# Row gathers ahead of writes, a zeroing transfer, mixer activations, output tiles and weight remainders at other places in one three-layer kernel

## The reference, cut to what matters

```python
# first block
sh1, sc1, gt1, sh2, sc2, gt2 = split(silu(c) @ w_ada + b_ada, 6)
h = rms_norm(x, g_mix) * (1 + sc1) + sh1
z = h @ w_in                                       # 1024 -> conv, LRU, attention parts
u = silu(layer_norm(causal_dw_conv(cv_v * sigmoid(cv_g), 31 taps)))        # 256 wide
r = rg_lru(causal_dw_conv(lr_x, 4 taps)) * gelu(lr_y)                      # 384 wide
o = rms_norm(gla_chunked(q, k, v, log_sigmoid(g) / 16)) * silu(og)         # 4 heads of 96
x = x + gt1 * (concat(u, r, o) @ w_out)
h = rms_norm(x, g_ffn) * (1 + sc2) + sh2
x = x + gt2 * hier_moe(h)     # best of 4 groups, top 2 of its 4 experts; SwiGLU of width 512
x = rms_norm(x, g_final)
# second block, twice
x = x + 0.5 * swiglu(rms_norm(x))                  # width 2816
qa, ka, va, qs, ks, vs, zg = split(rms_norm(x) @ w_in)
o_na = neighbourhood_attention(norm(qa), norm(ka), va)      # 8 heads of 64
o_sw = sliding_window_gqa(norm(qs), norm(ks), vs, sink)     # 8 heads, 2 of keys
g = sigmoid(zg + b_gate)
x = x + (g[0] * (o_na @ w_branch_na) + g[1] * (o_sw @ w_branch_sw)) @ w_out
x = x + 0.5 * swiglu(rms_norm(x))
```

## Time and profile before

| | |
|---|---|
| three executions | 3095.05, 3088.95, 3094.0 us (median 3094.0) |
| profiled execution | 3086.77 us, its span 3085.0 us |
| mean granted TensorE clock | 0.961 |
| PE busy | 2838.5 us, 92% of the span |
| PE weight load, DVE, ACT, POOL busy | 2421.5, 1970.5, 1457.9, 136.6 us |
| chain that ended last | PE 72%, issue 9%, DVE 8%, ACT 5%, DMA 4%, POOL 2% |
| largest DMA issues | raw x220 and m_raw x192 of 512 KB, 3.3 and 6.5 us to landing |

### The profile page before, as it was taken

The page is one execution under the profiler, slowest core; times in us unless marked ns, Lnnn a source line. Parts: engine busy times, 40 slices in busy tenths (PEclk is TensorE's granted clock), DMA queues, the critical chain, the costliest instruction groups (busy, mean ns, idle before and its releaser), DMA issues.

```text
span 3085.0 us, 46431 instructions
## 1 busy us (share of the span) xinstructions
PE 2838.5 (92%) x16210; PEld 2421.5 (78%) x16210; DVE 1970.5 (64%) x2847; ACT 1457.9 (47%) x2190; POOL 136.6 (4%) x76
## 2 busy tenths in 40 slices
PE   5989869999599998999999999999998999999999
PEld 3765557777399986777889998899876777889987
DVE  7532167887589754454369975899654544479964
ACT  3251337777455433554345543655334553355532
POOL 2430200110000000000000000000000000000000
PEclk8998969999799999999999999999998999999999
DMA  7710239998222233111323223232223112323322
GB/s 288 278 41 1 96 120 339 362 355 327 100 98 99 93 102 116 41 48 48 110 89 108 98 93 116 77 108 98 88 89 116 44 38 75 103 96 110 103 82 101
DMA packets 95245, 377.60 MB, mean 122 GB/s; under 512 B 10832, under 2 KB 11104, under 8 KB 92896
## 3 DMA queue, kind: packets, MB, share of 16 engines
q1 hardware_dynamic: 89072, 348.69, 32.4%
q0 software_dynamic: 4608, 16.78, 1.4%
q10 hardware_dynamic: 1456, 10.66, 0.9%
HBM read 363.50 MB, written 16.78 MB: 123 GB/s over the span
## 4 chain that ended last, share of the span: by engine, by line
PE 72%; issue 9%; DVE 8%; ACT 5%; DMA 4%; POOL 2%; ACTq 0%; SPq 0%; DVEq 0%; POOLq 0%
PE pb L1305 11%; PE pb L1306 11%; PE pb L1307 11%; PE pb L1634 9%; PE pb L1636 9%; PE pb L1635 9%; DMA rows<-h_rows,h_idx 3%; PE pb L1830 2%; PE pb L1801 2%; PE pb L1378 1%; POOL w_lo L566 1%; PE pb L1814 1%; ACT SP L1186 1%; DMA m_raw<-in_moe_stream 1%; DVE SP L2615 1%
## 5 line engine op out<-in xcount | busy, mean ns | idle before, releaser
L1634 PE MATMUL pb<-bl,g_wh 128*128 128x256 f32 x2464 | 703.4, 285 | 30.2 <-DVE bl L2384 14.4
L1635 PE MATMUL pb<-bh,g_wl 128*128 128x256 f32 x2464 | 699.2, 284 | 0.0
L1636 PE MATMUL pb<-bh,g_wh 128*128 128x256 f32 x2464 | 699.1, 284 | 0.0
L1634 PEld LDWEIGHTS pb<-bl,g_wh 128*128 128x128 f32 x2464 | 474.9, 193 | 35.2 <-issue 24.3
L1635 PEld LDWEIGHTS pb<-bh,g_wl 128*128 128x128 f32 x2464 | 475.0, 193 | 1.8 <-issue 1.7
L1636 PEld LDWEIGHTS pb<-bh,g_wh 128*128 128x128 f32 x2464 | 474.9, 193 | 0.0
L1305 PE MATMUL pb<-hl,w_hi 128*128 128x512 f32 (+1 forms) x688 | 287.9, 419 | 49.8 <-DVE hl L1944 17.6
L624 ACT ACTIVATE w_hi<-raw 128x1024 fp32r<-128x1024 f32 x196 | 206.0, 1054 | 219.6 <-PE pb L1307 192.6
L2421 DVE TENSOR_TENSOR w_lo<-raw,w_hi 128x1024 fp32r<-128x1024 f32 x164 | 200.5, 1223 | 144.6 <-ACT w_hi L624 143.4
L1306 PE MATMUL pb<-hh,w_lo 128*128 128x512 f32 (+1 forms) x688 | 275.4, 400 | 0.0
L1307 PE MATMUL pb<-hh,w_hi 128*128 128x512 f32 (+1 forms) x688 | 275.0, 400 | 0.0
(11 more groups left out here) (420 smaller groups left out, 5445.8 us busy)
## 6 DMA issues: line engine op xcount, KB each, us to landing
raw<-in_wstream SPq DMA_DIRECT2D x220, 512.0 KB, 3.3
m_raw<-in_moe_stream SPq DMA_DIRECT2D x192, 512.0 KB, 6.5
g_own<-in_gu_stream SPq DMA_DIRECT2D x44, 768.0 KB, 4.2
raw<-in_gu_stream SPq DMA_DIRECT2D x44, 768.0 KB, 4.2
ada_ring<-in_ada SPq DMA_DIRECT2D x8, 2048.0 KB, 8.4
g_own<-in_gu_stream SPq DMA_DIRECT2D x44, 256.0 KB, 3.1
hidf<-in_gu_stream SPq DMA_DIRECT2D x44, 256.0 KB, 3.1
adaw<-in_ada SPq DMA_DIRECT2D x4, 2048.0 KB, 23.2
```

The lines of the kernel that those rows point to most:

```text
L1634: pe.matmul(o, lh, rl, start=first and k == 0, stop=False, skip_group_check=True)
L1635: pe.matmul(o, ll, rh, start=False, stop=False, skip_group_check=True)
L1636: m = pe.matmul(o, lh, rh, start=False, stop=k == 3, skip_group_check=True)
```

## The change

Six edits, none of which adds or drops a computation.

1. POOL: `put(E - 3)` stands behind `gather(E)` where `put(E - 2)` stood, so each gather is issued before the write that stood ahead of it.
2. SP: the zeroing transfer is issued after the load of chunks 22 and 23, not before that of chunk 16.
3. ACT: the z loop is written out, and sigmoid, silu and gelu stand in its iterations 6, 7 and 8.
4. DVE: `u_pad` is made ahead of the wait for the end of the projection and of the first LRU convolution.
5. PE: the `w_out` product takes its tiles in `MIX_ORDER` (LRU, linear attention, convolution), with a wait for each tile; the first tile takes bank 0 last. `w_out` is laid out to match in DRAM.
6. DVE, second block: remainders of weights stand at other places among the norms, and `scores(3)` stands ahead of a remainder.

```diff
+MIX_ORDER = (*range(NU, NMIX), *range(NU))
@@ SP
+            stream((ADA - ADA1) // ADA_EACH, C_WOUT // 2 + 1)
             sp.dma_start(y_rows[0:2 * T, :], moe_stream[...]...).then_inc(y_zero, 16)
-            stream((ADA - ADA1) // ADA_EACH, C_L // 2)
+            stream(C_WOUT // 2 + 1, C_L // 2)
@@ POOL
                 gather(E)
-                if E >= 2:
-                    put(E - 2)
-            for E in range(NE - 2, NE):
+                if E >= 3:
+                    put(E - 3)
+            for E in range(NE - 3, NE):
                 put(E)
@@ ACT
-            with act.Fori(0, NZ // 2) as j:
+            for j in range(NZ // 2):
                 for s in range(2):
...
+                if j >= 6:
+                    for s in range(2):
+                        act.wait_ge(z_evac[s], 1 + 7)
+                    at, n, function = ((Z_CG, NU, ACT.Sigmoid), (Z_OG, GH, ACT.Silu), (Z_LY, NR, ACT.Gelu_apprx_tanh))[j - 6]
+                    act.activation(z[:, at:at + n, :], z[:, at:at + n, :], function).then_inc(z_act, 1)
...
-            for s in range(2):
-                act.wait_ge(z_evac[s], 1 + 11)
-            act.activation(z[:, Z_CG:Z_CG + NU, :], z[:, Z_CG:Z_CG + NU, :], ACT.Sigmoid).then_inc(z_act, 1)
...
@@ PE
-            pe.wait_ge(mix_lo, 2 + GH)
-            for i in range(NMIX):
+            for i, tile in enumerate(MIX_ORDER):
                 s = i % 2
                 chunk(C_WOUT // 2 + i // 2, s)
-                r = slice(0, DV if i >= NU + NR else P)
-                for m in range(KD):
-                    ins = mm3(pb[m][:], w_hi[s][r, m, :], w_lo[s][r, m, :], mixh[r, i, :], mixl[r, i, :],
+                pe.wait_ge(mix_lo, 2 + GH if tile < NU else max(1, tile - NU - NR + 2))
+                r = slice(0, DV if tile >= NU + NR else P)
+                for m in (*range(1, KD), 0) if i == 0 else range(KD):
+                    if i == 0 and m == 0:
+                        pe.wait_ge(ln_act, 2)
+                    ins = mm3(pb[m][:], w_hi[s][r, m, :], w_lo[s][r, m, :], mixh[r, tile, :], mixl[r, tile, :],
@@ DVE, mixer
-            dve.wait_ge(z_evac[0], 1 + 5)
-            dve.wait_ge(z_evac[1], 1 + 5)
+            dve.memset(u_pad[:, :, 0:CONV_K - 1], 0.0).then_inc(u_ready, 1)
+            dve.wait_ge(z_act, 1)
+            dve.tensor_tensor(u_pad[...], z[:, Z_CV:Z_CV + NU, :], z[:, Z_CG:Z_CG + NU, :],
+                              ALU.mult).then_inc(u_ready, 1)
             dve.wait_ge(w_used, C_WIN + N_WIN)
-            dve.memset(u_pad[:, :, 0:CONV_K - 1], 0.0).then_inc(u_ready, 1)
             for t in range(NR):
-                if t == 1:
-                    dve.wait_ge(z_act, 1)
-                    dve.tensor_tensor(u_pad[...], z[:, Z_CV:Z_CV + NU, :], z[:, Z_CG:Z_CG + NU, :],
-                                      ALU.mult).then_inc(u_ready, 1)
@@ DVE, attention
                 low(kb + 1, 0)
+                low(kb + 1, 1)
                 qk(n0, htmp[:, 0, :], root[:], ksn[:], False).then_inc(ks_done, 1)
...
-                low(kb + 1, 1)
                 low(hb + 1, 0)
+                low(hb + 1, 1)
                 normed_q(n0 + 1)
-                low(hb + 1, 1)
+                normed_k(n0 + 1)
                 low(hb + 2, 0)
-                normed_k(n0 + 1)
...
                     normed(2)
+                    scores(3)
                     low(pr + 2, 1)
-                    scores(3)
                     normed(3)
@@ layout of w_out
-    parts = [win, wout, blocks_k(pad_to(rt, D, P))[None]]
+    parts = [win, wout[list(MIX_ORDER)], blocks_k(pad_to(rt, D, P))[None]]
```

More of the change, by code:

```diff
@@ L680, in _ @@
                     act.wait_ge(w_used, C_WIN + 2 * j + s + 1)
-                    act.activation(z[:, bass.ds(2 * j + s, 1), :].rearrange("p a t -> p (a t)"), pb[1 + s][:],
-                                   ACT.Copy).then_inc(z_evac[s], 1)
+                    act.activation(z[:, 2 * j + s, :], pb[1 + s][:], ACT.Copy).then_inc(z_evac[s], 1)
+                if j >= 6:
[3 more added lines that the diff above has]
+                    act.activation(z[:, at:at + n, :], z[:, at:at + n, :], function).then_inc(z_act, 1)
             n = C_WIN + NZ - 1
@@ L699, in _ @@
                 hi(n // 2 + 2, i)
-            for s in range(2):
-                act.wait_ge(z_evac[s], 1 + 11)
-            act.activation(z[:, Z_CG:Z_CG + NU, :], z[:, Z_CG:Z_CG + NU, :], ACT.Sigmoid).then_inc(z_act, 1)
-            act.activation(z[:, Z_OG:Z_OG + GH, :], z[:, Z_OG:Z_OG + GH, :], ACT.Silu).then_inc(z_act, 1)
-            act.activation(z[:, Z_LY:Z_LY + NR, :], z[:, Z_LY:Z_LY + NR, :], ACT.Gelu_apprx_tanh).then_inc(z_act, 1)
             act.preload_act_table_set(LN_EXP)
@@ L2000, in _ @@
             dve.scalar_tensor_tensor(gs[:, 1, :], modv[:, 24:32], 1.0, V("g_ffn", 0, KD), ALU.add, ALU.mult).then_inc(mod_ready, 1)
-            dve.wait_ge(z_evac[0], 1 + 5)
-            dve.wait_ge(z_evac[1], 1 + 5)
+            dve.memset(u_pad[:, :, 0:CONV_K - 1], 0.0).then_inc(u_ready, 1)
+            dve.wait_ge(z_act, 1)
+            dve.tensor_tensor(u_pad[:, :, CONV_K - 1:], z[:, Z_CV:Z_CV + NU, :], z[:, Z_CG:Z_CG + NU, :],
+                              ALU.mult).then_inc(u_ready, 1)
             dve.wait_ge(w_used, C_WIN + N_WIN)
-            dve.memset(u_pad[:, :, 0:CONV_K - 1], 0.0).then_inc(u_ready, 1)
             for t in range(NR):
-                if t == 1:
-                    dve.wait_ge(z_act, 1)
-                    dve.tensor_tensor(u_pad[:, :, CONV_K - 1:], z[:, Z_CV:Z_CV + NU, :], z[:, Z_CG:Z_CG + NU, :],
-                                      ALU.mult).then_inc(u_ready, 1)
                 xz, y = z[:, Z_LX + t, :], mt[:, t, :]
```

## The result

The changed kernel took 3018.86 us (median of 4, 3017.35 to 3026.66), the kernel before 3093.33 (median of 4, 3088.95 to 3095.05). The ratio is 0.9766, 95% interval 0.9747 to 0.9786: 74.5 us faster. The profiled execution has a span of 3017.7 us instead of 3085.0, so the two traces differ by 67.3 us; the terms are held against these 67.3. A second measurement gave 3019.23.

A forecast was written before the change was run, and what follows sets the result against it. PE, busy 92% of the span, was taken as the bound, with DMA close in the experts. Terms 9.9 + 6.0 + 8.3 + 11.4 + 13.8 + 6.1 = 55.5 us off the mean 3091.2 gave 3036; 8-in-10 range 3014 to 3052.

The forecast's parts named there:

- second rival: Experts' stage: PE sets the pace, so all 26 us of waiting for rows come off; time 3021, chance 0.12.
- Experts: Gathers issued ahead of writes remove PE's wait for rows: 7.8 us in the stage plus up to 3.6, 11.4 us.
- upper bound from the wait itself: Experts: PE's 23.4 us of waits for rows plus 2.6 us of lost clock, 26 us at most.
- the last expert: End of the experts: its rows' remainder is ready at 744.7 but PE takes it at 748.36, up to 3.6 us more.
- LRU gates: After the projection: activations inside the z loop and early `u_pad` let the gates start at 204.0 instead of 209.96, 6.0 us.
- third rival: z loop: the functions push ACT's roundings and the activations' 8.3 us come on PE's path; time 3044, chance 0.05.
- Zeroing: Projection: with the transfer later, PE's 7.41 us of idle time and 2.5 us of half speed go, 9.9 us.
- Tiles: Output product: LRU tiles first remove PE's 6.99 us wait for the convolution and 1.3 us of half speed, 8.3 us.
- Attention starts: Second block: moving a remainder from ahead of PE's work saves 6.9 us in each of two layers, 13.8 us.
- Pairs: Attention heads: `scores(3)` ahead of a remainder saves 0.8 us for each of 8 pairs, a little less at layer ends, 6.1 us.
- Slower rival: Experts: a gather issued mid-expert holds up that expert's weights, up to 8.0 us in each of 13; time 3151, chance 0.04.

## Why the prediction was right or wrong

It said 3036 with 3014 to 3052; 3018.9 is inside, at the lower end. The forecast itself (3028 to 3044, 0.62) missed. The time is that of the second rival (3021, 0.12), which also had the mechanism of the experts right; the range holds the result only because it was widened to take in a part of that rival.

- **Experts, the step that failed.** The prediction took "the DMA engines are unused 0.03 of 260 us, so the stage can shrink by 7.8 us". It shrank by 25.3 (27.4 alone). The share of busy DMA time did not tell how much more the engines could carry: the rate rose from 361 to 397 GB/s while the share went from 0.96 to 1.01, and with half the loads of the changed kernel the stage was only 3.8 us shorter. The upper bound from the wait itself, 23.4 + 2.6 = 26, was near, though the edit alone went 1.4 over it. The 3.6 us for the last expert were too many as well: 1.6 came at that place. Of the two rows the wait row should have had the weight, since it names what PE stood still for.
- **LRU gates, mis-sized.** "Nothing in the diff touches that block": 4.29 against 2.32 us had a cause, POOL beside it, and the edit moved its price about. 1.6 instead of 6.0. With POOL's remainders moved away the same edits gain 7.4 to 7.9 us over the kernel before in three traces; that is the 8.0 which the prediction gave for a first block as quick as its sister, and did not take. The third rival (ACT late in the z loop) wasn't there: 0.67 us to spare.
- **Zeroing** 11.6 (10.3 undone) against 9.9, the chain from the late load to PE right, but 6.4 of the 10.3 are engine time and 3.9 the queue. **Tiles** 8.7 against 8.3, the cover held; a little more of the half-speed stretch went. **Attention starts** 12.9 against 13.8, bound by the root as said. **Pairs** 7.3 against 6.1: 0.7 instead of 0.8 a pair, plus a half-speed stretch that wasn't in the sum.
- **Slower rival** (a gather in the middle of an expert holds the weights): absent. The loads cost 3.8 us in the stage in all, and the landing of a gather got shorter, not longer.

The sum without the two wrong terms is 38.1 predicted and 40.5 measured.

The 7.2 us between 67.3 in the two traces and 74.5 in the medians lie in the choice of executions: the kernel before was profiled in one that was 6.6 us quicker than its median (3086.8 against 3093.3), the changed kernel in one that was 0.7 slower (3019.6 against 3018.9). What makes executions of one kernel differ stays open. Of nine executions of the kernel before, the quickest (3085.23) had a mean granted clock of 0.963 and the slowest (3093.35) one of 0.960, which fits the half speed behind short waits, below.

## What to carry to other kernels

A DMA share near 1 next to an idle PE does not say that DMA is the limit: here the share stood at 0.96 at 361 GB/s and the rate still rose by a tenth, so price the wait that PE actually has and check the limit by cutting the bytes. When one instruction of a group takes twice the time of its sisters, look at what POOL does in that stretch before you move work around it; the price follows the neighbour. A small transfer that is wanted soon should be issued before anything that waits for a later event on the same queue.

## What the hardware showed that was not expected

- **Half speed behind a wait of 2 us comes or doesn't.** The same kernel ran twice, with the same wait of 1.93 us. In the first trace and in the second one:

```profile
1191.62 3.12 PE L1804 MATMUL pb<-kn,qn 64*128 64x256 f32 x8 [1.93 <-DVE kn L2567]
```

```profile
1188.98 1.99 PE L1804 MATMUL pb<-kn,qn 64*128 64x256 f32 x8 [1.93 <-DVE kn L2567]
```

  From 1195 to 1200 us the granted clock was 0.58 in the first and 1.00 in the second, and the stretch at 1.2 instead of 2.4 GHz made the start of the attention 4.8 us longer in the first. It is also why a term of 3 us can't be read from one pair of traces, and it may be why executions of one kernel lay 9 us apart (3014.5 to 3023.2).
- **DVE beside POOL.** A group of three DVE instructions that takes 2.32 us took 6.49 while POOL made two remainders in 5.12 us, and 2.32 when these were moved. `u_pad` took 2.84 or 1.16.
- **A large transfer delays loads on another queue.** Beside the 4.19 MB of the zeroing, issued by ACT, loads of 512 KB issued by SP landed in 13.5 us instead of 3.2.
- **Close to 400 GB/s for one core.** The experts' stage held 397 GB/s over 220 us.
